# Hybrid decoder layer step: gathered expert rows turned next to the hidden product, and stored with even features first

## The reference, cut to what matters

```python
xp = layer_norm(alpha * xp + mp[:, 2] * op, ln1_g[l], ln1_b[l])
vp = modulate(xp, mp[:, 3], mp[:, 4])          # layer_norm(xp) * (1 + scale) + shift
f = hmoe(jnp.concatenate([vp..., vs...]), w_rg, b_rg, w_re, b_re, w_gate, w_up, w_down)
# hmoe: lg = v @ w_rg + b_rg; le = v @ w_re + b_re; the best of 4 groups, the best 2 of its 8 experts
#       for each expert e and the rows x routed to it:
#           h = silu(x @ w_gate[e]) * (x @ w_up[e]);  y = h @ w_down[e]
#       each row gets the sum of its two y, weighted by its gates
```

## Time and profile before

| | |
|---|---|
| median of 3 timed runs | 1611.13 us |
| lowest and highest | 1605.96 and 1612.22 us |
| the profiled execution | 1596.19 us |
| its span | 1594.6 us |
| mean granted TensorE clock | 0.943 of full speed |
| TensorE busy (products) | 1380.7 us, 87% |
| VectorE busy | 957.0 us, 60% |
| ScalarE busy | 556.3 us, 35% |
| GpSimd busy | 301.7 us, 19% |
| mean DMA rate | 230 GB/s |

### The profile page before, as it was taken

The page is one execution under the profiler, slowest core; times in us unless marked ns, Lnnn a source line. Parts: engine busy times, 40 slices in busy tenths (PEclk is TensorE's granted clock), DMA queues, the critical chain, the costliest instruction groups (busy, mean ns, idle before and its releaser), DMA issues.

```text
span 1594.6 us, 37025 instructions
## 1 busy us (share of the span) xinstructions
PE 1380.7 (87%) x13489; PEld 1027.2 (64%) x13489; DVE 957.0 (60%) x1696; ACT 556.3 (35%) x849; POOL 301.7 (19%) x318
## 2 busy tenths in 40 slices
PE   4799999979999997799997399999979999977672
PEld 4688989979888886587786255555545555543330
DVE  6755545758998888786686743423442424443459
ACT  4222223435556664631321032413341423343210
POOL 4000002210000000000000124343433433423300
PEclk8999999999999999899999599999999999997896
DMA  9666306553333444732335889985999859999852
GB/s 287 208 232 225 123 27 197 179 154 108 108 121 111 144 136 166 268 108 68 94 112 217 318 312 360 369 333 204 403 407 365 331 212 356 401 376 408 312 216 103
DMA packets 169600, 366.06 MB, mean 230 GB/s; under 512 B 16040, under 2 KB 94944, under 8 KB 166328
## 3 DMA queue, kind: packets, MB, share of 16 engines
q1 hardware_dynamic: 150472, 308.19, 53.0%
q0 software_dynamic: 18480, 54.80, 9.9%
q10 hardware_dynamic: 576, 2.10, 0.4%
HBM read 324.15 MB, written 45.73 MB: 232 GB/s over the span
## 4 chain that ended last, share of the span: by engine, by line
PE 38%; DVE 5%; DMA 4%; issue 4%; SPq 3%; ACT 3%; DVEq 2%; ACTq 0%; POOLq 0%
PE PS L2101 15%; PE PS L1976 10%; PE PS L2119 6%; DMA ring<-in_w_down_dram 3%; ACT ring L1919 2%; PE PS L2155 2%; PE PS L2110 2%; PE PS L2089 1%; PE PS L2007 1%; PE PS L2042 1%; SPq L1621 1%; SPq L1601 1%; PE PS L1999 1%; SPq L1668 1%; DVEq L2440 0%
## 5 line engine op out<-in xcount | busy, mean ns | idle before, releaser
L886 PE MATMUL PS<-big 128*128 128x352 f32 x2592 | 433.7, 327 | 1.6 <-DVE big L1140 1.6
L886 PEld LDWEIGHTS PS<-big 128*128 128x128 f32 x2592 | 422.3, 190 | 10.4 <-issue 6.7
L2101 PE MATMUL PS<-ring,arena 128*32 128x256 f32 x5248 | 314.4, 393 | 13.9 <-DVE arena L2421 13.9
L2101 PEld LDWEIGHTS PS<-ring,arena 128*32 128x32 f32 x5248 | 176.0, 113 | 128.4 <-issue 36.9
L1919 ACT ACTIVATE ring<-ring 128x1024 f32 x124 | 121.0, 1046 | 134.4 <-SPq L1644 87.8
L1756 POOL DMA_INDIRECT arena<-v_d,icur x84 | 103.1, 1227 | 332.4 <-DVE icur L2433 206.2
L2119 PE MATMUL PS<-ring,arena 128*32 128x256 f32 x2624 | 158.6, 382 | 1.1 <-DVE arena L2429 1.0
L2450 DVE COPY ring<-ring 128x1024 f32 x124 | 77.7, 689 | 100.3 <-SPq L1644 44.9
L1764 POOL DMA_INDIRECT f_d<-arena,scur x82 | 118.7, 1448 | 51.7 <-issue 43.9
L2421 DVE COPY arena<-PS 128x256 f32<-128x256 f32 x82 | 34.6, 422 | 130.4 <-PE PS L2089 130.4
L2119 PEld LDWEIGHTS PS<-ring,arena 128*32 128x32 f32 x2624 | 76.9, 109 | 53.6 <-DVE arena L2429 1.7
(11 more groups left out here) (428 smaller groups left out, 1866.3 us busy)
## 6 DMA issues: line engine op xcount, KB each, us to landing
ring<-in_w_gate_dram SPq DMA_DIRECT2D x32, 2048.0 KB, 10.5
ring<-in_w_up_dram SPq DMA_DIRECT2D x32, 2048.0 KB, 15.6
ring<-in_w_down_dram SPq DMA_DIRECT2D x32, 2048.0 KB, 13.0
arena<-in_w_ada_dram SPq DMA_DIRECT2D x16, 1024.0 KB, 6.6
arena<-in_w_in_dram SPq DMA_DIRECT2D x20, 512.0 KB, 7.8
upper<-in_w_ada_dram SPq DMA_DIRECT2D x8, 1024.0 KB, 11.7
upper<-in_w_in_dram SPq DMA_DIRECT2D x16, 512.0 KB, 3.9
arena<-acs_d SPq DMA_DIRECT2D x8, 1024.0 KB, 4.8
```

The lines of the kernel that those rows point to most:

```text
L886: mm = pe.matmul(PS[:, 3 * b + a, 0:CH], wss[b][:, i, k, :], us[:, j, k, a * CH:(a + 1) * CH], start=(k == 0 and (i, j) == PARTS[0]), stop ...
L2101: mm = pe.matmul(PS[32 * g:32 * g + 32, 3, 0:FH], xT[:, c, CAP * q:CAP * q + CAP], wcur[:, w:w + FH], start=(q == 0 and c == 0), stop=(q = ...
```

## The change

Four edits. `norms` writes `V` with its 512 even features first and then its 512 odd ones (on the decode tile by one more copy), and with it `v_d` and all gathered rows; the router's weights are loaded in the same order, by four DMAs in place of two. `x_turn` reads contiguous columns, and `gate_up` picks the parts of `xT` by the new order. On TensorE `x_turn(u+2)` stands between `h_turn(u)` and `gate_up(u+1)`. On VectorE `gather_rows(u+4)` stands at the head of the iteration and waits for the turn of unit u+2, whose buffer it reuses; before, that wait was `x_out`'s.

```diff
--- before.py
+++ after.py
@@ -1558,6 +1558,12 @@
         POS = {t: q for q, t in enumerate(ORDER)}
         QD = POS[NT]
 
+        def paired(x):
+            return x.rearrange("p (m c) -> p c m", c=2)
+
+        def apart(x):
+            return x.rearrange("p (c m) -> p c m", c=2)
+
         def rows_of(q):
             return DEC if q == QD else P
 
@@ -1603,7 +1609,9 @@
                         load_x(0)
                 load_x(1)
                 for dst, src in ((wr[:, :, 0:NG], w_rg[0]), (wr[:, :, NG:NG + NE], w_re[0])):
-                    sp.dma_start(dst, src.rearrange("(k p) n -> p k n", p=P)).then_inc(wr_loaded, 16)
+                    for c in range(2):
+                        sp.dma_start(dst[:, 4 * c:4 * c + 4, :], src.rearrange("(q p c) n -> c p q n", p=P, c=2)[c])\
+                            .then_inc(wr_loaded, 16)
                 sp.dma_start(brb[:, 0:NG], b_rg.to_broadcast([P, NG])).then_inc(wr_loaded, 16)
                 sp.dma_start(brb[:, NG:NG + NE], b_re.to_broadcast([P, NE])).then_inc(wr_loaded, 16)
 
@@ -2053,7 +2061,7 @@
 
                 for q in range(NTT):
                     if q == 2:
-                        pe.wait_ge(wr_loaded, 64)
+                        pe.wait_ge(wr_loaded, 96)
                     if q == QD:
                         out_decode(q)
                     else:
@@ -2086,7 +2094,7 @@
                     pe.wait_ge(xg_loaded[b], j * 16 + 16)
                     pe.wait_ge(xT_ready, u)
                     for c in range(2):
-                        mm = pe.transpose(PS[:, 0, P * c:P * c + P], xg[b][:, c::2], ident[:, :])
+                        mm = pe.transpose(PS[:, 0, P * c:P * c + P], xg[b][:, P * c:P * c + P], ident[:, :])
                     mm.then_inc(eT_mm, 1)
 
                 def gate_up(u):
@@ -2098,7 +2106,7 @@
                         for c in range(2):
                             for g in range(4):
                                 w = 4096 * (g // 2) + 1024 * q + 512 * c + FH * (g % 2)
-                                mm = pe.matmul(PS[32 * g:32 * g + 32, 3, 0:FH], xT[:, c, CAP * q:CAP * q + CAP],
+                                mm = pe.matmul(PS[32 * g:32 * g + 32, 3, 0:FH], xT[:, q % 2, CAP * (2 * c + q // 2):CAP * (2 * c + q // 2) + CAP],
                                                wcur[:, w:w + FH], start=(q == 0 and c == 0),
                                                stop=(q == QW - 1 and c == 1))
                         mm.then_inc(gu_mm, 1)
@@ -2128,14 +2136,14 @@
                 x_turn(1, 0, 1)
                 for u in range(2):
                     h_turn(u)
+                    x_turn(u + 2, 1, u)
                     gate_up(u + 1)
-                    x_turn(u + 2, 1, u)
                     down(u)
                 with pe.Fori(1, pairs) as j:
                     for b in range(2):
                         h_turn(j * 2 + b)
+                        x_turn(j * 2 + (b + 2), j + 1, b)
                         gate_up(j * 2 + (b + 1))
-                        x_turn(j * 2 + (b + 2), j + 1, b)
                         down(j * 2 + b)
                 h_turn(pairs * 2)
                 gate_up(pairs * 2 + 1)
@@ -2237,13 +2245,21 @@
                     else:
                         ve.wait_ge(v_stored, 16 * q)
                         ve.wait_ge(vt_mm, q)
-                    row(ve.scalar_tensor_tensor(out=V[0:r, :], in0=x[0:r, :], scalar=mv[0:r, 0:1],
-                                                in1=(V if q == QD else sc2)[0:r, :], op0=ALU.subtract, op1=ALU.mult))
+                    if q == QD:
+                        row(ve.scalar_tensor_tensor(out=V[0:r, :], in0=x[0:r, :], scalar=mv[0:r, 0:1], in1=V[0:r, :],
+                                                    op0=ALU.subtract, op1=ALU.mult))
+                    else:
+                        row(ve.scalar_tensor_tensor(out=apart(V), in0=paired(x), scalar=mv[:, 0:1], in1=paired(sc2),
+                                                    op0=ALU.subtract, op1=ALU.mult))
                     ve.wait_ge(lns_ready, 2 * q + 2)
                     row(ve.reciprocal(rstd[0:r, :], rstd[0:r, :]))
-                    ve.scalar_tensor_tensor(out=V[0:r, :], in0=V[0:r, :], scalar=rstd[0:r, :],
-                                            in1=(O if q == QD else sh2)[0:r, :], op0=ALU.mult, op1=ALU.add)\
-                        .then_inc(v_ready, 1)
+                    if q == QD:
+                        row(ve.scalar_tensor_tensor(out=O[0:r, :], in0=V[0:r, :], scalar=rstd[0:r, :], in1=O[0:r, :],
+                                                    op0=ALU.mult, op1=ALU.add))
+                        ve.tensor_copy(apart(V[0:r, :]), paired(O[0:r, :])).then_inc(v_ready, 1)
+                    else:
+                        ve.scalar_tensor_tensor(out=apart(V), in0=apart(V), scalar=rstd[:, :], in1=paired(sh2),
+                                                op0=ALU.mult, op1=ALU.add).then_inc(v_ready, 1)
 
                 for i in range(2):
                     wo_low(i)
@@ -2430,6 +2446,7 @@
                         .then_inc(hT_ready, 1)
 
                 def gather_rows(u, b):
+                    ve.wait_ge(eT_mm, u + -1)
                     ve.tensor_copy(icur[b][:, :], idxT[:, bass.ds(u, 1)]).then_inc(icur_ready, 1)
 
                 def scatter_rows(u, j, b):
@@ -2476,20 +2493,20 @@
                 gather_rows(3, 1)
                 ve.wait_ge(vector_once, IDXS_READY)
                 for u in range(2):
+                    gather_rows(u + 4, u)
                     h_out(u)
                     up_copy(u + 2, u + 1)
                     x_out(u + 2)
-                    gather_rows(u + 4, u)
                     scatter_rows(u, 0, u)
                     down_copy(u + 1)
                 ve.wait_ge(vector_once, CTL_READY)
                 pairs = ve.value_load(ctl[0:1, CTL_N:CTL_N + 1], min_val=NE // 2 - 1, max_val=(NE + NOV) // 2 - 1)
                 with ve.Fori(1, pairs) as j:
                     for b in range(2):
+                        gather_rows(j * 2 + (b + 4), b)
                         h_out(j * 2 + b)
                         up_copy(j * 2 + (b + 2), j * 2 + (b + 1))
                         x_out(j * 2 + (b + 2))
-                        gather_rows(j * 2 + (b + 4), b)
                         scatter_rows(j * 2 + b, j, b)
                         down_copy(j * 2 + (b + 1))
                 h_out(pairs * 2)
```

## The result

| | before | after |
|---|---|---|
| median of 6 timed runs, side by side | 1611.11 us | 1621.82 us |
| lowest and highest | 1605.96 and 1612.22 | 1618.13 and 1623.51 |
| ratio, 95% interval | | 1.0076 (1.0059 to 1.0092) |
| the profiled execution and its span | 1596.19, 1594.6 us | 1619.93, 1617.9 us |
| `h_turn` of the first and of the last unit | 931.40, 1516.18 | 931.32, 1539.06 |

The changed kernel is slower by 0.8%, where 0.6% faster was forecast. The spans of the two profiled executions differ by 23.3 us, 22.9 of it between the first and the last `h_turn`: 607.7 us instead of 584.8.

The account below looks back on a forecast made before the run. TensorE's order was taken to bound plain units, ScalarE copying ones, and the weight stream stretches of short experts. Savings of 11.0 and 2.5 less losses of 1.0, 1.2 and 0.9 took 1611.13 to 1600.7 us, range 1593 to 1609.5.

Parts of the forecast that it names:

- (c): GpSimd (POOL) queue in the unit loop: gather now between two scatters, started and needed some 4 us sooner; cost 0.
- plain unit: Loop unit in which no new expert's weights are copied, bound by TensorE's order: 6.26 us to become 5.91, saving 0.35.
- or if copying units change at all: Condition for being wrong: units copying a new expert's gate weights, bound by ScalarE, were to stay at 6.8 us, saving 0.
- The rival for slower, gathers as the bound: Unit loop: gathers taking beyond 9.5 us hold the products, each microsecond costing one per unit; about 1624 us, chance 0.05.
- the sum: All terms over the kernel: -11.0 - 2.5 + 1.0 + 1.2 + 0.9 = -10.4 us.
- Start, +1.0: Loop start: unit 2's gather needed 3.9 us sooner but cannot be asked for sooner; 1.0 us lost (0 to 3.9).
- Strided operations, 0: VectorE in norms, storing even features first: two operations per tile read with 8-byte stride; 0 taken, 0 to 1.4 us possible.
- Router's weights, +0.9: Ahead of the mixer output loads: two more DMAs issued by SyncE at 0.43 us each, exposed; +0.9 us.
- Waits on VectorE, +1.2: Unit loop, where two new experts follow each other: late x_out holds the turn and VectorE's next product; 1.2 us lost.

Follow-up runs that it names:

- the third set: The changed kernel, unaltered, rerun against the kernel before (1599.33 us) on a chip without freezes: 0.9938, 1589.64 us; variants ran beside it.
- the fourth: The changed kernel, unaltered, run again against the kernel before (1607.62 us) on a chip with freezes: 1.0071, 1619.59 us; variants ran beside it.
- second set: The changed kernel with each gather held until three quarters of gate_up are multiplied, against the kernel before (1610.18 us): 0.9877, 1591.47 us.
- the first and the fifth: Sets on one chip: parts of the change alone (storage alone 0.9993), then the changed kernel with gathers held (0.9945, 0.9955), each against the kernel before.

## Why the prediction was wrong

- **The step that failed** is (c): "On POOL the gather of unit u+4 now stands behind the scatter of u-1 and ahead of the scatter of u, each about 1.0 us ... 0." The place was right, 0.30 us behind the scatter, and so was the gather being in time. What was not asked is what two transfers in direct succession do to the engines that do not wait for them. On the kind of chip on which the comparison was made, that costs 0.4 to 1.0 us in each plain unit without a down copy and 0.7 to 1.0 in most copying ones, and together 29.5 us between the first and the last `h_turn` (607.7 against 578.2 us in the third set). The forecast gain is gone, and the medians came out 10.7 us apart the wrong way. The kernel before pays some of it on such a chip too. Its profile on record, with plain units of 6.26 us, looks like one of the other kind: the 1% by which its timed median stood above that profile, which the prediction carried over as it was, probably holds this loss, since that kernel takes 8 to 11 us more on the chips that freeze.
- **"or if copying units change at all"** was the condition that came true: they went to 7.8 us, with ScalarE's copies broken apart.
- The rival for slower, gathers as the bound, is refuted: `x_turn` waited for a gather twice, 1.5 us in all. Its sign came from another mechanism.
- **The rest of the sum** can be read where nothing freezes, in the third set. There the change gives 9.7 us between the medians (1599.33 and 1589.64); the sum was 10.4. A plain unit takes 5.90 us, forecast 5.91. The gathered rows' loads last 141 ns each, and `down` follows `gate_up` directly. Copying units keep a median of 6.9. The loop is 8.2 us shorter (578.2 instead of 586.4): 9.0 less in the 28 plain units and 3.2 less in the 16 with a down copy, but 2.8 more in the copying ones, where nothing was forecast, and 0.9 more in the first. So the nearness of 9.7 to 10.4 is in part luck.
- **Start, +1.0:** the first `x_turn` of the loop waited 1.26 us for its gather there, and 0.85 and 1.02 in the other two profiles of the changed kernel. The whole first unit lost more in two of three pairs of profiles: 8.83 against 7.89 us in the third set, but 8.42 and 9.71 against 6.26 on record and in the fourth. Where it took 6.26 us the mean granted clock from 931 to 945 us was 1.00, in the others 0.76 to 0.88.
- **Strided operations, 0:** both are at 1285 ns for 128x1024, as the contiguous ones are; the first of them in the groups of the changed kernel, third set:

```profile
L2252 DVE SCALAR_TENSOR_TENSOR arena<-arena,mv 128x1024 f32<-128x1024 f32 x8 | 10.3, 1285 | 0.3
```

  The rule on 16-byte cachelines in the Trainium skill's SBUF — State Buffer holds for them. TensorE's loads go the other way: with the rows contiguous each takes 141 ns instead of 204, which made 0.32 us a pair. The storage alone brought the plain unit from 6.26 to 6.19 us.
- **Router's weights, +0.9:** not seen as such. The first `h_turn` comes at 931.4 to 933.1 us in four profiles of the old storage and at 931.3 to 936.5 in 16 of the new, means 932.0 and 934.0. A mean loss of 2 us ahead of the loop is likely, larger than forecast, and within the spread of single profiles.
- **Waits on VectorE, +1.2:** where a down copy starts late, `down` now waits for hT, which the turn behind `gate_up` used to cover: 10.1 us in the loads of `down` in the third set, 1.8 in the kernel before beside it. This term was sized too small.

## What to carry to other kernels

Before a transfer is moved on a queue, look at what stands directly ahead of it there, and at engines that do not wait for either. If idle times with "issue" as cause appear in a dense stretch, look for what GpSimd issued in the 1.5 us before, and at whether other engines go on at the same moment. And compare a kernel with its own profile on the same chip: a variant that shows no stall proves nothing until the unvaried kernel, beside it, shows one.

## What was not expected of the hardware

- Two indirect transfers of GpSimd, 1.02 us each and 0.30 us apart, stop TensorE, ScalarE and VectorE from going on with their instructions on some chips, until 1.4 to 1.5 us after the start of the second. Apart by 1.8 us they did not (second set), nor with a plain transfer of the same bytes in the place of the first, 0.55 us ahead. In the kernel before, 0.86 us apart in the order gather, scatter, they did not hold TensorE either; ScalarE was 0.12 us late.
- Of five sets on four chips, two showed it and three did not. The same kernels were met with and without it: the changed one, the one before, and the one with the gather ahead (0.9965 and 1.0094). Whether it is the chip itself or something set up on it once per set is open: one chip was met in two sets, the first and the fifth, both times without freezes, and none with both outcomes. Which part stands still is open too. Units without weight traffic had it as well.
- Where VectorE makes its down copy of 2.29 us, the pair costs nothing even on such a chip. Scatter and gather are 0.30 us apart there too, but the scatter lasts until the copy is over, and the gather starts at 3.6 us or later, mostly at 4.1 to 4.9, when TensorE is at `down`. The freeze itself is not gone: in the unit of the changed kernel with the earliest gather, 3.58 us in, ScalarE's copy of the hidden product (`hb_out`) starts 4.94 us into the unit, 1.36 behind the gather's start, where it is 4.32 in the third set. The unit takes 5.90 us all the same:

```profile
1268.57 1.02 POOL L1764 DMA_INDIRECT arena<-v_d,icur  x1 [0.31 <-issue]
1269.93 0.38 ACT L1907 ACTIVATE arena<-PS 128x256 f32<-128x256 f32 x1 [4.19 <-PE PS L2109]
```
